# A channel transform in three passes of rounded high and low parts, with the low parts of both operands written by the VectorE

## The reference

```python
xg = xb.astype(f32).reshape(bsz, L, G_B, GW_B)
fr = jnp.fft.fft2(xg, axes=(1, 3), norm='ortho').real
yb = jnp.einsum('blgi,gij->blgj', fr, w_four.astype(f32)).reshape(bsz, L, W_B) + b_four.astype(f32)
y = jnp.concatenate([ya.astype(h.dtype) * jax.nn.silu(za),
                     yb.astype(h.dtype) * jax.nn.silu(zb)], axis=-1)
```

## Time and profile before

| what | value |
|---|---|
| time, median of 3 runs | 2097.31 us (2096.49 to 2098.36) |
| the profiled execution's own time | 2094.5 us |
| its span, first to last instruction | 2092.9 us |
| mean granted TensorE clock | 0.992 |
| TensorE busy | 97% of the span |
| VectorE, ScalarE, GpSimd busy | 50%, 31%, 6% |
| the 8 `to_tokens` in the trace | 144 records, 331.9 to 579.0 us |

### The profile page before, as it was taken

One profiled execution on the slowest core, in us unless ns is written; L12 is line 12 of the kernel. 1 busy time (PEld: TensorE's weight loads), 2 busy tenths in 40 slices (PEclk: granted clock), 3 DMA queues, 4 the chain that ended last, 5 costly groups with the idle time before them and its releaser, 6 DMA issues.

```text
span 2092.9 us, 28311 instructions
## 1 busy us (share of the span) xinstructions
PE 2024.3 (97%) x11724; PEld 1892.5 (90%) x11724; DVE 1051.7 (50%) x1620; ACT 650.4 (31%) x823; POOL 126.5 (6%) x111
## 2 busy tenths in 40 slices
PE   5999999999999999979999999999999999999998
PEld 3999998999988888879999999999999999998886
DVE  4688886535353474753434334344343433645344
ACT  5677774221334453211111111111111211214322
POOL 0032322000200010000000000000000000000001
PEclk8999999999999999999999999999999999999999
DMA  7212214533146443131220312203122031316554
GB/s 284 76 43 66 73 37 98 173 133 127 62 149 185 156 162 104 42 108 36 91 59 21 113 36 92 58 21 114 41 85 59 23 117 41 100 44 201 171 172 136
DMA packets 215145, 204.61 MB, mean 98 GB/s; under 512 B 13202, under 2 KB 186874, under 8 KB 213874
## 3 DMA queue, kind: packets, MB, share of 16 engines
q1 hardware_dynamic: 210994, 190.52, 29.7%
q0 software_dynamic: 3680, 12.29, 1.7%
q10 hardware_dynamic: 352, 0.10, 0.0%
HBM read 172.14 MB, written 30.59 MB: 97 GB/s over the span
## 4 chain that ended last, share of the span: by engine, by line
PE 79%; issue 8%; POOL 3%; ACT 3%; DVE 3%; DMA 3%; ACTq 0%; POOLq 0%; SPq 0%; DVEq 0%
PE psum_groups L126 37%; PE psum_groups L1146 18%; PE psum_groups L1762 10%; PE psum_groups L1743 3%; PE psum_extra L1734 3%; PE psum_groups L1745 2%; POOL tanh_then_state L571 2%; DMA w_raw<-in_w_in_e 1%; PE psum_groups L936 1%; POOL mixed_y L576 1%; PE psum_groups L143 1%; PE psum_groups L926 1%; PE psum_extra L950 1%; PE psum_groups L1703 1%; PE psum_groups L1714 1%
## 5 line engine op out<-in xcount | busy, mean ns | idle before, releaser
L126 PE MATMUL psum_groups<-h_hi,w_hi 128*128 128x384 f32 x1896 | 449.5, 345 | 14.6 <-DVE h_lo L480 6.0
L126 PE MATMUL psum_groups<-h_lo,w_hi 128*128 128x384 f32 x1896 | 434.5, 337 | 0.0
L126 PE MATMUL psum_groups<-h_hi,w_lo 128*128 128x384 f32 x1896 | 434.2, 337 | 0.0
L126 PEld LDWEIGHTS psum_groups<-h_hi,w_hi 128*128 128x128 f32 x1896 | 339.1, 188 | 25.5 <-issue 13.6
L126 PEld LDWEIGHTS psum_groups<-h_lo,w_hi 128*128 128x128 f32 x1896 | 340.7, 188 | 0.0
L126 PEld LDWEIGHTS psum_groups<-h_hi,w_lo 128*128 128x128 f32 x1896 | 340.2, 188 | 0.0
L1146 PE MATMUL psum_groups<-w_out,y_tile_hi 128*128 128x512 f32 x1008 | 317.5, 394 | 0.0
L1146 PEld LDWEIGHTS psum_groups<-w_out,y_tile_hi 128*128 128x128 f32 x1008 | 189.6, 188 | 42.5
L2028 DVE SCALAR_TENSOR_TENSOR state<-state,head_decay,psum_extra 128x257 f32<-128x257 f32 x112 | 54.1, 483 | 287.5 <-PE psum_groups L1745 285.5
L1146 PE MATMUL psum_groups<-w_out,y_tile_lo 128*128 128x512 f32 x504 | 198.1, 393 | 0.0
L1762 PE MATMUL psum_groups<-w_hi,h_hi 128*128 128x256 f32 x576 | 165.2, 287 | 12.1 <-DVE w_lo L111 9.4
(11 more groups left out here) (311 smaller groups left out, 2484.7 us busy)
## 6 DMA issues: line engine op xcount, KB each, us to landing
w_raw<-in_w_in_o SPq DMA_DIRECT2D x65, 512.0 KB, 4.2
y_tile_raw<-y_scratch SPq DMA_DIRECT2D x126, 256.0 KB, 3.0
w_raw<-in_w_in_e SPq DMA_DIRECT2D x32, 512.0 KB, 4.1
w_mod_rest<-in_w_mod SPq DMA_DIRECT2D x4, 4096.0 KB, 14.8
y_scratch<-mixed_y POOLq DMA_DIRECT2D x16, 576.0 KB, 3.6
decay_matrix<-gate_rows SPq DMA_DIRECT2D x8, 1152.0 KB, 7.7
q_carry<-gate_rows SPq DMA_DIRECT2D x8, 1152.0 KB, 6.4
y_scratch<-out_gate SPq DMA_DIRECT2D x8, 1152.0 KB, 5.2
```

What stands on the lines that cost most here:

```text
L126: ins = pe.matmul(PS[:, group, j, 0:JW], w[:, slot, k * P:(k + 1) * P], h(k0 + k)[:, j * JW:(j + 1) * JW], start=start and k == 0 and m == ...
```

## The change

`XB` and `CW` become rounded high parts (the same two ACT copies, with an F32R output). DVE writes the low parts: `PSUM - high`, straight from the PSUM group that ACT copied from, 128x1152 for the tokens and 128x256 for the weights. `to_tokens` makes three passes for each tile of tokens. A semaphore `xb_lo` counts the low parts, and TensorE waits for it where it waited for the copies: before the first gate r product of the recurrence's last block, before `modulation`, and before `to_tokens`. For group 0 the low part of the tokens is written in the recurrence's last block, and the low part of the weights comes behind that block.

```diff
-    XB = sb("xb", [P, T], at=mix_zone)
-    xb_out = sem("xb_ready")
-    CW = sb("channel_weights", [P, 2, P], at=mix_zone)
+    XB = sb("xb_hi", [P, T], F32R, at=mix_zone)
+    xb_out = sem("xb_hi_ready")
+    CW = sb("channel_weights_hi", [P, 2, P], F32R, at=mix_zone)
...
+    XBL0 = sb("xb_lo_first", [P, T], F32R, at=list(mix_zone))
+    xb_lo = sem("xb_and_channel_weights_lo_ready")
...
                             elif isinstance(i, int) and i == KC - 1:
-                                pe.wait_ge(xb_out, 1)
+                                pe.wait_ge(xb_lo, 1)
...
                 ch.link(dve.scalar_tensor_tensor(GZ[:], ZT[:], 1.0, ZH[:], ALU.add, ALU.mult))
+                if last:
+                    dve.wait_ge(xb_out, 1)
+                    dve.tensor_tensor(by_bank(XBL0[:]), PS[:, 0, :, 0:JW], by_bank(XB[:]).bitcast(F32), ALU.subtract
+                                      ).then_inc(xb_lo, 1)
...
-            def to_tokens(first, last, bank, done):
+            def to_tokens(i, first, last, bank, done):
                 for t in range(first, last):
-                    ins = pe.matmul(bank(t - first), XB[:, t * P:(t + 1) * P], CW[:].rearrange("p a n -> p (a n)"),
-                                    start=True, stop=True, skip_group_check=True)
+                    cols = slice(t * P, (t + 1) * P)
+                    for m, (x, w) in enumerate(((XB, CW), (XBL if i else XBL0, CW), (XB, CWL))):
+                        ins = pe.matmul(bank(t - first), x[:, cols], w[:].rearrange("p a n -> p (a n)"),
+                                        start=m == 0, stop=m == 2, skip_group_check=True)
                 ins.then_inc(done, 1)
...
                 pe.wait_ge(wm_in, 16 * (q + 1))
-                pe.wait_ge(cw_out, i + 1)
+                pe.wait_ge(xb_lo, 2 * i + 1)
...
-                pe.wait_ge(xb_out, i + 1)
-                pe.wait_ge(cw_out, m * 2 + slot + 1)
+                pe.wait_ge(xb_lo, 2 * i + 2)
...
+            def channel_weights_lo(i):
+                dve.wait_ge(cw_out, i + 1)
+                if i:
+                    dve.wait_ge(ub_done, i)
+                dve.tensor_tensor(CWL[:].rearrange("p a n -> p (a n)"), PX[:, 1, 256:512],
+                                  CW[:].rearrange("p a n -> p (a n)").bitcast(F32), ALU.subtract).then_inc(xb_lo, 1)
+
+            def xb_rest(i):
+                dve.wait_ge(xb_out, i + 1)
+                dve.tensor_tensor(by_bank(XBL[:]), PS[:, 0, :, 0:JW], by_bank(XB[:]).bitcast(F32), ALU.subtract
+                                  ).then_inc(xb_lo, 1)
...
             def group(i):
-                if not isinstance(i, int) or i:
+                if i:
                     w_split_lo(dve, i + KC, 1)
+                channel_weights_lo(i)
+                if i:
+                    xb_rest(i)
                 if not isinstance(i, int) or i:
                     outputs(i - 1, isinstance(i, int) and i == 1)
```

More of the change, by code:

```diff
@@ L837, in fourier @@
     def fourier():
+        z = [lru_zone[0] + 4 * 2 * P * 4]
+        XBL = sb("xb_lo", [P, T], F32R, at=z)
+        CWL = sb("channel_weights_lo", [P, 2, P], F32R, at=z)
         WM = sb("w_mod_rest", [P, KC, D], at=[zone])
@@ L972, in group @@
                     pe.wait_ge(mod_rows, i - CHUNK0 + 1)
-                to_tokens(0, 6, lambda t: PS[:, 0, t // 2, t % 2 * 256:t % 2 * 256 + 256], ua_done)
-                to_tokens(6, 9, lambda t: PX[:, t // 2, t % 2 * 256:t % 2 * 256 + 256], ub_done)
+                to_tokens(i, 0, 6, lambda t: PS[:, 0, t // 2, t % 2 * 256:t % 2 * 256 + 256], ua_done)
+                to_tokens(i, 6, 9, lambda t: PX[:, t // 2, t % 2 * 256:t % 2 * 256 + 256], ub_done)
                 if not first:
```

## The result

The changed kernel takes 2099.81 us (median of 22 runs, 2097.86 to 2103.56) beside 2096.78 us for the kernel before (22 runs, 2093.21 to 2099.39). The ratio is 1.0017, 95% interval 1.0011 to 1.0023: slower by 0.17%, some 3.6 us, less than the 0.2% that the prediction had named as the bound of "no change". The forecast was +7.2 us; the measured median lies 0.3 us above the lower end of the stated range. The profiled execution has its own time of 2099.02 us and a span of 2097.5 us, 4.6 us more than before.

The account below looks back on a forecast made before the run. TensorE, busy for 97% of the span, was taken as the bound. 14.1 + 2.1 - 3.65 - 0.5 - 1.81 - 3.0 = +7.2 us, on the median of 2097.31, gave 2104.5 us, range 2099.5 to 2108.

Parts of the forecast that it names:

- The case that the forecast named: Recurrence end and `to_tokens(0)`: two TensorE waits with half clock behind each, +5 to +9.5 us, chance 0.67.
- slower by over 0.2%: Whole kernel: outcome class of more than +4.2 us, chance 0.78.
- within 0.2%: Whole kernel: outcome class about indistinguishable from no change, 0.2% being 4.2 us, chance 0.17.
- The first wait: Recurrence's last block: first gate r product waits for DVE's low part, 5.5 us late; with half clock 7.4 us.
- The second wait: `to_tokens(0)`: waits for the weights' low part behind DVE's last scan, starting at 346.1, 14.1 us later.
- `to_tokens(0)` at half clock: First `to_tokens`, behind its wait for the weights' low part: +2.1 us.
- Given back ahead of `to_tokens(1)`: `token_transform(0)`: no longer waits 2.06 us nor loses 1.6 us to half clock, -3.65 us.
- Given back ahead of `channel_weights(2)`: TensorE's wait for `Z` of group 1 vanishes, -1.81 us; `to_tokens(1)` saves another 0.5.
- The saving of a group: Each `to_tokens`: 27 F32R matmuls take 3.2 us instead of 3.70, saving 0.5 us; groups 2 to 7 give -3.0.
- Rival 2: Both seam waits: no half clock, +2.2 us (2099.5), or behind one wait alone, +3.5 to +5; chance 0.18.
- Rival 3: Steady groups: low parts late in groups 1, 6 and 7 too, 3.3 us more, +10.5 us (2107.8); chance 0.10.
- Rival 4: `to_tokens(0)`: weights' subtraction not held behind the scans, start at 337.4, -4 us (2093.4); chance 0.05.

Follow-up runs that it names:

- e7: The changed kernel with filler matmuls on TensorE in both waits (28 and 34, into an unread PSUM bank); ratio 0.9999 to the kernel before, stage +0.92 us.
- e1: The changed kernel with DVE writing the tokens' low part of group 0 ahead of `GZ`; ratio 0.9990 to the kernel before, stage -0.71 us.
- e5: The changed kernel with plain F32 operands and one plain pass, all DVE subtractions and waits kept; ratio 1.0046 to the kernel before, stage +9.82 us.
- e2: The changed kernel with the first weights' low part written between the last block's two scans; ratio 1.0011 to the kernel before, stage +1.88 us.
- e3: The changed kernel with tokens' low part ahead of `GZ` and weights' low part between the scans; ratio 0.9987 to the kernel before, stage -0.95 us.
- e6: The kernel before with rounded operands and three high-by-high passes, without low parts, subtractions or their waits; ratio 0.9980 to the kernel before, stage -2.26 us.
- e4: The changed kernel with group 0 left in plain F32, groups 1 to 7 as changed; ratio 0.9989 to the kernel before, stage -2.39 us.
- e8: The changed kernel with group 0 plain and x(2)'s weight tile issued ahead of the 4 MB load; ratio 0.9966 to the kernel before, stage -5.62 us.

## Why the prediction was right, and where it was mis-sized

The direction, the two places and their causes were right; the size was not: +7.2 us forecast, 3.0 us by the medians, 3.6 by the ratio, +4.20 in the stage. That the time still lies in the range is in part luck. The lower end, 2099.5, was put there for a case without any half clock, which did not happen, and 2099.81 is 0.3 us above it. The case that the forecast named, two half clocks and +5 to +9.5, came true in its mechanism and not in its size, and the class held likeliest, slower by over 0.2% (chance 0.78), was missed; "within 0.2%" had 0.17. By its own steps, in the profiled pair:

- **The first wait**: 5.5 us forecast, 319.34 - 313.80 = 5.54. ACT's second gate i tanh: 7.4 late forecast, 324.36 - 317.56 = 6.80. The half clock ended at 322.8, before all 18 matmuls were through; I had taken nearly all of them at half clock. e7 has the wait and not the clock.
- **The second wait**: `to_tokens(0)` 14.1 late forecast, 345.40 - 331.93 = 13.47, all of the difference from the step before. DVE's 1.35 and 0.43 us were 1.36 and 0.42.
- **`to_tokens(0)` at half clock**: +2.1 forecast, (352.07 - 337.14) - 13.47 = 1.46. The half clock ended at 350.1, 22 of 27 matmuls in. Both half-clock terms were mis-sized by 0.6 us each, in the same direction, and in another execution they may fall otherwise: in e1 all 27 ran at half clock.
- **Given back ahead of `to_tokens(1)`**: 3.65 forecast; 14.93 - (369.01 - 358.09) = 4.0.
- **Given back ahead of `channel_weights(2)`**: with group 1's saving 2.3 forecast; 10.92 - (384.81 - 376.46) = 2.6. The load came at 377.0, 3.9 us later than before, not 7.4; either hides. The forecast took the load to move with the recurrence's end. That end moved by 6.8 us (last scan copy at 344.84 for 338.05), but POOL then needed 5.3 instead of 8.0 us from the start of its sum to the end of its product, so that SP issued the 4 MB load at 350.38 for 346.32.
- **The saving of a group**: this is the single term that missed most. 0.5 forecast, 0.67 measured; groups 2 to 7 gave (384.81 - 376.46) - (595.97 - 591.75) = 4.1 instead of 3.0. I had priced the 27 matmuls (3.2 forecast, 3.3 measured) and not what stands next to them, the 0.20 of z(i) and the 0.07 of the token transform.

Summed: 13.47 + 1.46 - 4.01 - 2.57 - 4.13 = +4.2 for the stage, 3.0 less than forecast: 1.3 of that are the half-clock terms, 1.1 the saving of groups 2 to 7, 0.6 the two terms given back. No wait behind the stage took any of it: the span grew by 4.6. The median of many executions moved by 3.0, the ratio gives 3.6; a profiled pair is one draw of the half-clock terms.

Rival 2 (no half clock) was priced at +2.2; e7 shows +0.92 for it, lower by what eight groups give at 0.17 us each (1.4). Rival 3, low parts late in groups 1, 6 and 7, is refuted by the changed kernel's own timeline, which has no idle time ahead of `to_tokens` in any of these groups, and by the 1.36 us that DVE's reads took; e5's period of 37.13 us says the same of group 3. Rival 4's condition, the weights' low part not held behind all the scans, is what e2 nearly brings about, and its price was wrong: `to_tokens(0)` starts at 341.27 instead of 337.4, since the low part still stands behind the first direction's scan and the first wait still delays that, and of the gains counted behind it in full (3.65 and 1.81 us) waits of 0.69 and 1.46 us come back. e2 ends at +1.88 and not at -4. Only where the first wait is shortened (e1, and e3 with both moves) does the stage come out on the faster side, -0.71 and -0.95. What I had missed in these was the load ahead of `channel_weights(2)`: the forecast used it as a wait that vanishes because TensorE is late, and did not draw the reverse, that what is won in the seam runs into it again (e2, e3), in e3 with clock on top.

The Trainium skill (TensorE: Matmul & The Clock Gate, the table of the two states) names the two levels, 1.2 and 2.4 GHz. The traces agree: within a stretch the windows show a granted clock of 1.00 or 0.50. Idle times of 1.50 (e1), 1.81 (before), 2.34 (e2) and 2.48 us (e6) left the clock at 1.00, and 2.06 (before), 2.38 (e3), 2.56 (e4), 3.24 (e3) and 3.94 us (e6) brought it to 0.50, so the length of the idle time alone does not decide.

## What to carry to other kernels

Where an operand's low part is written by an engine that runs in order, ask what stands ahead of it there: a 1.36 us subtraction behind a wait for another engine cost 4.9 us of the stage, and moving it ahead of that wait brought them back (e1). A saving that repeats in every step of a stage can be lost in the steps ahead of a wait for something with a time of its own, a load above all (e4, e6); look for that wait first, and move the load (e8). Price a wait of TensorE with the clock behind it, and a pass with its neighbours: time from one fixed point of the loop to the same point in the next turn shows both.

## What the runs showed of the hardware that was not expected

- A change between plain and rounded matmuls has a price of its own. Behind nine plain matmuls z(2) took 12.69 us, behind rounded ones 12.49; the first rounded matmul behind plain ones now stands in `to_tokens`, where it takes 405.68 - 405.48 = 0.20 us instead of the 0.12 of those behind it.
- The wait ahead of `channel_weights(2)` left the clock at 1.00 with 1.81 us (before), and with 2.56 us (e4) it was halved, which cost 1.6 us in the work behind it. Length alone is no guide, though: 2.38 us (e3) was followed by 0.50 and 2.48 us (e6) was not. And the half clock can begin when work has started again: in e3 1.1 us after the 2.38 us of idle time had ended, in e6 1.3 us after the 3.94 us.
- POOL's last sums and products of the recurrence took longer with DVE at work beside it, and DVE too: the product took 2.41 us in the changed kernel and 4.27 in e2, the first two butterflies 2.36 and 4.61. From DVE's last scan copy to SP's issue of the 4 MB load it took 5.5 us in the changed kernel, e1 and e5, where DVE stands idle until `Z` is there, and 7.4 to 8.3 us before, in e2 and in e3, where the butterflies run meanwhile. No run changes that alone, so the cause is read from the rows and not shown.
- DVE's subtraction with one operand in PSUM and an F32R output of 1,152 columns took 1.34 to 1.36 us in every profile that has it, as the eight with a plain output did: the format does not show in the time.
